# FFN entry of a two-layer hybrid encoder trunk: weight operands 0 to 3 split ahead of the last units, sums of x in another order, first products in two parts

## The reference, cut to what matters

```python
def _swiglu(x, w_in, w_out):
    g, u = jnp.split(x @ w_in, 2, axis=-1)
    return (jax.nn.silu(g) * u) @ w_out

# for each of two layers, x is 512 prompt rows and 8 x 16 sample rows of 1024
x = x + 0.5 * _rmsnorm(_swiglu(_rmsnorm(x, g[0]), w_ffn_in[l, 0], w_ffn_out[l, 0]), g[1])
x = x + _rmsnorm(Mixer_l(_rmsnorm(x, g[2])), g[3])
x = x + 0.5 * _rmsnorm(_swiglu(_rmsnorm(x, g[4]), w_ffn_in[l, 1], w_ffn_out[l, 1]), g[5])
```

## Time and profile before

| | |
|---|---|
| median of 3 runs | 2647.21 us (2640.1 to 2655.18) |
| profiled execution, own time | 2651.45 us |
| its span | 2649.5 us |
| TensorE matmul busy | 2458.7 us (93%) |
| VectorE busy | 1714.9 us (65%) |
| ScalarE busy | 1194.7 us (45%) |
| mean granted TensorE clock | 0.966 of full |

### The profile page before, as it was taken

One profiled execution on the slowest core, in us unless ns is written; L12 is line 12 of the kernel. 1 busy time (PEld: TensorE's weight loads), 2 busy tenths in 40 slices (PEclk: granted clock), 3 DMA queues, 4 the chain that ended last, 5 costly groups with the idle time before them and its releaser, 6 DMA issues.

```text
span 2649.5 us, 37614 instructions
## 1 busy us (share of the span) xinstructions
PE 2458.7 (93%) x13907; PEld 2197.0 (83%) x13907; DVE 1714.9 (65%) x2819; ACT 1194.7 (45%) x2159; POOL 117.9 (4%) x177
## 2 busy tenths in 40 slices
PE   5999999998899899999989999999997687999998
PEld 4999987976767799988789998777775467999887
DVE  6777647676555877745687774663246858777546
ACT  4445435344344554534555453442233435555444
POOL 1000001100001000000100000100000010000000
PEclk9999999999889999999999999999996889999999
DMA  3333334322203223233432324443251032332335
GB/s 114 90 92 84 98 129 164 104 72 73 76 1 127 64 80 96 80 116 131 150 80 80 96 65 143 139 139 127 68 157 54 1 121 71 90 87 80 109 129 175
DMA packets 259140, 261.89 MB, mean 99 GB/s; under 512 B 25568, under 2 KB 214000, under 8 KB 258977
## 3 DMA queue, kind: packets, MB, share of 16 engines
q1 hardware_dynamic: 254224, 243.83, 30.4%
q0 software_dynamic: 4464, 14.80, 1.6%
q10 hardware_dynamic: 288, 1.10, 0.1%
HBM read 249.11 MB, written 10.58 MB: 98 GB/s over the span
## 4 chain that ended last, share of the span: by engine, by line
PE 77%; DVE 14%; ACT 4%; issue 3%; DMA 1%; POOL 1%; SPq 0%; DVEq 0%; ACTq 0%; POOLq 0%
PE ps L844 12%; PE ps L846 12%; PE ps L845 12%; PE ps L902 5%; PE ps L903 5%; PE ps L904 5%; PE ps L1278 3%; PE ps L1279 2%; PE ps L1280 2%; PE ps L961 2%; PE ps L963 2%; PE ps L962 2%; PE ps L1754 1%; DVE w_all L591 1%; DVE xb L707 1%
## 5 line engine op out<-in xcount | busy, mean ns | idle before, releaser
L844 PE MATMUL ps<-xb,w_all 128*128 128x320 f32 x2400 | 751.2, 313 | 54.7 <-DVE w_all L591 33.9
L845 PE MATMUL ps<-xb,w_all 128*128 128x320 f32 x2400 | 747.9, 312 | 0.0
L846 PE MATMUL ps<-xb,w_all 128*128 128x320 f32 x2400 | 747.8, 312 | 0.0
L844 PEld LDWEIGHTS ps<-xb,w_all 128*128 128x128 f32 x2400 | 456.3, 190 | 62.6 <-issue 46.8
L491 DVE TENSOR_TENSOR w_all<-raw,w_all 128x1024 fp32r<-128x1024 f32 (+1 forms) x204 | 207.9, 1020 | 401.2 <-ACT w_all L501 212.7
L845 PEld LDWEIGHTS ps<-xb,w_all 128*128 128x128 f32 x2400 | 456.4, 190 | 0.0
L846 PEld LDWEIGHTS ps<-xb,w_all 128*128 128x128 f32 x2400 | 456.2, 190 | 0.0
L485 ACT ACTIVATE w_all<-raw 128x1024 fp32r<-128x1024 f32 (+1 forms) x204 | 182.3, 895 | 485.1 <-PE ps L904 260.0
L591 DVE TENSOR_TENSOR w_all<-raw,w_all 128x512 fp32r<-128x512 f32 x404 | 277.8, 690 | 146.9 <-ACT w_all L584 145.9
L584 ACT ACTIVATE w_all<-raw 128x512 fp32r<-128x512 f32 x404 | 253.3, 629 | 182.3 <-PE ps L846 138.9
L902 PE MATMUL ps<-w_all 128*128 128x512 f32 x528 | 205.9, 390 | 0.9 <-DVE w_all L506 0.9
(11 more groups left out here) (355 smaller groups left out, 4002.4 us busy)
## 6 DMA issues: line engine op xcount, KB each, us to landing
raw<-in_w_ffn_out SPq DMA_DIRECT2D x176, 512.0 KB, 3.3
raw<-in_w_ffn_in SPq DMA_DIRECT2D x120, 512.0 KB, 5.0
gain<-in_w_ffn_in SPq DMA_DIRECT2D x56, 512.0 KB, 4.9
raw<-in_w_in_odd SPq DMA_DIRECT2D x56, 256.0 KB, 2.7
raw<-in_w_out_even SPq DMA_DIRECT2D x16, 512.0 KB, 3.5
raw<-in_w_out_odd SPq DMA_DIRECT2D x16, 512.0 KB, 3.4
gain<-in_norm_g POOLq DMA_DIRECT2D x12, 512.0 KB, 7.4
raw<-in_w_in_even SPq DMA_DIRECT2D x24, 256.0 KB, 2.6
```

The source lines that it names most:

```text
L844: nc.tensor.matmul(dst, wl, xh[:, k, :], start=first, stop=False, skip_group_check=True)
L845: nc.tensor.matmul(dst, wh, xl[:, k, :], start=False, stop=False, skip_group_check=True)
L846: mm = nc.tensor.matmul(dst, wh, xh[:, k, :], start=False, stop=(k == HK - 1), skip_group_check=True)
```

## The change

Four things are done at each FFN entry. The gate tiles of pairs 0 and 1 are loaded before both up tiles, operands 0 and 1 are split before the last unit of the matmul in front (k == rows - 2) and operands 2 and 3 beside it (k == rows - 1). T1 is made in three pieces, by token tiles 2, 3 and 4, the last straight from PSUM; T3 goes from ahead of product 4 to step 7, T4 from step 8 to step 9, and s4 of pairs 0 and 1 from step 4 and 5 to steps 8 and 9. ScalarE copies token tile 4 in two halves around the high part of T1. Products of pair 0 multiply by the high part of x first (8 matmuls) and wait for its low part only before the last 4. In FFN 0 lambda and `wf` move to the norms in front, and tile 3 is transposed before product 3 in every FFN.

```diff
-            for c in range(pairs):
-                if name[0] == "A" and c == 2:
+            if name[0] == "A":
+                for which in range(2):
+                    for c in range(2):
+                        tile(c, which)
+                        if name == "A0" and which == 0:
+                            load_x(sp, NP - 1 + c)
...
-            if name == ("P5" if j < 2 else "P2"):
+            if name == ("P7" if j < 2 else "P2"):
                 dve.wait_ge(op_lo, NPROD * f + PLACE["P2", j] + 1)
...
+        def dve_t1(dve, f, t):
+            xt0 = XT["pre%d" % (BEFORE[f] + 1)]
+            c0, c1 = max(t * P, HT) - HT, (t + 1) * P - HT
+            if t == 2:
+                dve.wait_ge(xb_lo_done, 7 * f + 1)
+            if t < NT - 1:
+                dve.wait_ge(xt_hi, xt0 + t + 1)
+                b12 = xs[:, 0:HK, HT + c0:HT + c1]
             else:
+                dve.wait_ge(xt_ps, xt0 + NT)
+                b12 = xt_src(t, 0)[:, 0:HK, :]
+            t1 = nc.vector.tensor_tensor(xs[:, 0:HK, c0:c1], b12, xs[:, 0:HK, c0:c1], ALU.subtract)
+            if t == NT - 1:
+                t1.then_inc(t12_done, 1)
...
+        def dve_first_t(dve, f):
+            dve_first_sums(dve, f, 0)
+            dve_t1(dve, f, 2)
+            dve_first_sums(dve, f, 1)
+            dve_t1(dve, f, 3)
+            dve_operand(dve, f, 4)
+            dve_t1(dve, f, 4)
+            dve_operand(dve, f, 5)
+            dve_s2(dve, f, 0)
+            dve_xb(dve, f, "T1")
+            dve_t2(dve, f)
+            dve_s2(dve, f, 1)
...
-        ACT_X = {4: ["T1"], 6: ["T2"], 8: ["T3"], 10: ["T4"], 12: ["B22"]}
+        X_FRONT = {8: "T3", 10: "T4", 12: "B22"}
...
+            act_operand(act, f, 4)
+            act_operand(act, f, 5)
+            xt0 = XT["pre%d" % (BEFORE[f] + 1)]
+            act.wait_ge(xt_ps, xt0 + NT)
+            nc.scalar.activation(xs[:, HK:, 4 * P:], xt_src(4, HK), ACT.Copy)
+            act_xb(act, f, "T1")
+            nc.scalar.activation(xs[:, 0:HK, 4 * P:], xt_src(4, 0)[:, 0:HK, :], ACT.Copy).then_inc(xt_hi, 1)
+            for i in range(RING, NPROD + RING + 3):
+                if i in X_FRONT:
+                    act_xb(act, f, X_FRONT[i])
                 if 0 <= i - RING < NPROD:
                     act_after(act, f, i - RING)
-                if i < NPROD:
+                if 5 < i < NPROD:
                     act_operand(act, f, i)
+                if i == 6:
+                    act_xb(act, f, "T2")
...
-            for i in range(AHEAD, NPROD + RING + 4):
-                if i == 4:
-                    for j in range(2):
-                        dve_first_sums(dve, f, j)
-                    dve.wait_ge(xt_hi, XT["pre%d" % (BEFORE[f] + 1)] + NT)
-                    dve_t(dve, f, "T1")
-                    dve_t(dve, f, "T3")
-                    dve_xb(dve, f, "T1")
-                if i == 5:
-                    dve_t(dve, f, "T2")
-                if i == 6:
-                    dve_xb(dve, f, "T2")
-                if i == 8:
-                    dve_t(dve, f, "T4")
-                    dve_xb(dve, f, "T3")
+            for i in range(6, NPROD + RING + 4):
                 if i < NPROD:
                     dve_operand(dve, f, i)
                     dve_sums(dve, f, i)
+                if i == 6:
+                    dve_xb(dve, f, "T2")
+                if i == 7:
+                    dve_t3(dve, f)
+                if i == 9:
+                    dve_t4(dve, f)
+                if i in X_FRONT:
+                    dve_xb(dve, f, X_FRONT[i])
...
+                if i == AHEAD - 1:
+                    pe_xt(pe, pre_, 3, 3)
                 if i == AHEAD:
-                    pe_xt(pe, pre_, 3, 3)
                     pe_xt(pe, pre_, 4, 4)
...
+                if j == 0:
+                    for k in range(HK):
+                        wh, wl = hi[:, k * P:(k + 1) * P], lo[:, k * P:(k + 1) * P]
+                        nc.tensor.matmul(dst, wl, xh[:, k, :], start=fresh and k == 0, stop=False, skip_group_check=True)
+                        nc.tensor.matmul(dst, wh, xh[:, k, :], start=False, stop=False, skip_group_check=True)
+                    pe.wait_ge(xb_lo_done, 7 * f + XB_ORDER.index(XOF[name]) + 1)
+                    for k in range(HK):
+                        wh = hi[:, k * P:(k + 1) * P]
+                        mm = nc.tensor.matmul(dst, wh, xl[:, k, :], start=False, stop=(k == HK - 1), skip_group_check=True)
...
+            f = FFN_PRE.get("pre%d" % (p + 1))
+            if f is not None and k == rows - 1:
+                act_operand(act, f, 2)
...
+            if f is not None and k == rows - 2:
+                act_operand(act, f, 0)
+                act_operand(act, f, 1)
+            if f is not None and k == rows - 1:
+                act_operand(act, f, 3)
+                if rows == KD:
+                    act_xb_first(act, p)
```

More of the change, by code:

```diff
@@ L379, in tile @@
                 sp_unit(sp, u0 + 2 * c + which, None, wv[:, :, which * stride + c * P:which * stride + (c + 1) * P])
-            for c in range(pairs):
-                if name[0] == "A" and c == 2:
[L384 to L387, removed]
+            if name[0] == "A":
[4 more added lines that the diff above has]
+                            load_x(sp, NP - 1 + c)
+                f = int(name[1])
+                if f:
+                    sp.wait_ge(m_out, 5 * (BEFORE[f] + 1))
+                sp.wait_ge(tok_ready, READY["pre%d" % (BEFORE[f] + 1)] + NT)
+            for c in range(2 if name[0] == "A" else 0, pairs):
                 tile(c, 0)
-                if name == "A0" and c < 2:
-                    load_x(sp, NP - 1 + c)
                 tile(c, 1)
@@ L606, in dve_first_sums, with dve_s2 @@
             nc.vector.tensor_tensor(a21, a21, a22, ALU.add).then_inc(s1_done, 1)
+        def dve_s2(dve, f, j):
+            a11, a12, a21, a22 = quarters(f, j)
+            dve.wait_ge(op_lo, NPROD * f + PLACE["P5", j] + 1)
+            dve.wait_ge(s3_done, KF * f + j + 1)
+            nc.vector.tensor_tensor(a21, a22, a11, ALU.subtract).then_inc(s2_done, 1)
         def dve_sums(dve, f, i):
@@ new lines, in dve_t2, with dve_t3 @@
+        def dve_t2(dve, f):
+            dve.wait_ge(xb_lo_done, 7 * f + 3)
+            dve.wait_ge(xt_hi, XT["pre%d" % (BEFORE[f] + 1)] + NT)
+            nc.vector.tensor_tensor(xs_quarter(0, 0), xs_quarter(1, 1), xs_quarter(0, 0), ALU.subtract).then_inc(t12_done, 1)
+        def dve_t3(dve, f):
+            dve.wait_ge(t12_done, 2 * f + 1)
+            dve.wait_ge(xt_hi, XT["pre%d" % (BEFORE[f] + 1)] + NT)
+            nc.vector.tensor_tensor(xs_quarter(0, 1), xs_quarter(1, 1), xs_quarter(0, 1), ALU.subtract).then_inc(t34_done, 1)
@@ L840, in pe_pairs_ffn @@
                 xh, xl = xb[:, XB[XOF[name]]], xb[:, XB[XOF[name]] + 1]
[L841 to L846, removed]
+                fresh = name in ("P1", "P2", "P5")
+                if j == 0:
[7 more added lines that the diff above has]
+                        mm = nc.tensor.matmul(dst, wh, xl[:, k, :], start=False, stop=(k == HK - 1), skip_group_check=True)
+                else:
+                    for k in range(HK):
+                        wh, wl = hi[:, k * P:(k + 1) * P], lo[:, k * P:(k + 1) * P]
+                        nc.tensor.matmul(dst, wl, xh[:, k, :], start=fresh and k == 0, stop=False, skip_group_check=True)
+                        nc.tensor.matmul(dst, wh, xl[:, k, :], start=False, stop=False, skip_group_check=True)
+                        mm = nc.tensor.matmul(dst, wh, xh[:, k, :], start=False, stop=(k == HK - 1), skip_group_check=True)
                 mm.then_inc(prod_mm, 1)
@@ L957, in pe_second_group @@
                         pe.wait_ge(m_out, 5 * p + 1)
+                        pe.wait_ge(ss_m_done, 5 * p + 1)
                     for n in range(2):
@@ L1034, in act_norm_first @@
                     act_xt(act, "pre%d" % (p + 1), t, t)
-                    if t == 2:
+                    if f is not None and t == 2 and rows == KF:
                         act_xb_first(act, p)
+            if f is not None and k == rows - 2:
[5 more added lines that the diff above has]
+                    act_xb_first(act, p)
         def act_xb_first(act, p):
@@ L1049, in act_norm_rest @@
             f = FFN_PRE.get("pre%d" % (p + 1))
-            if f is not None:
-                for i in range(AHEAD):
-                    act_operand(act, f, i)
-            elif nxt:
+            if f is None and nxt:
                 for i in range(2):
@@ L1066, in act_norm_rest @@
                 act_hi(act, nxt[0] + 4, None, BW).then_inc(hi_done, 1)
-            act_xt(act, "pre%d" % (p + 1), 4, 4)
+            if f is None:
+                act_xt(act, "pre%d" % (p + 1), 4, 4)
         def act_norm_start(act):
@@ L1124, in dve_norm_first @@
         def dve_norm_first(dve, p, k, rows):
+            f = FFN_PRE.get("pre%d" % (p + 1))
+            if f is not None and k == rows - 1:
```

(18 more changed lines are left out.)

77 lines of the change are left out of this document (34 added, 43 removed).

## The result

The changed kernel takes 2663.9 us (median of 9 runs, 2662.58 to 2667.88) against 2647.21 us (9 runs, 2638.31 to 2655.18): ratio 1.0066, 95% interval 1.0053 to 1.0079. It is slower, by 0.5 to 0.8%. Its profiled execution took 2662.66 us, with a span of 2660.7 and a mean granted clock of 0.962.

What follows compares the result with a forecast made beforehand. TensorE bounds the kernel, except where it idles at FFN entries, which are VectorE lists. Product 8's +10.3 us and the clock's +6.0 make +16.3 on 2651.45, 2667.8; with that execution 4.2 above median, 2663.5 us, range 2645 to 2676.

Steps and rivals of the forecast that it cites:

- List position of product 8: At each FFN entry, product 8 starts 24.3 us behind VectorE's first weight sum, not 20.5: 3.8 us later.
- Start of the lists: When VectorE's list begins at each entry: FFN 0 -5.35 us, FFN 1 -1.4, FFN 2 +2.55, FFN 3 -0.65.
- The clock: Longer idle time ahead of product 8 brings the low clock to products 8 and 9: +6.0 us over four entries.
- Rival 1: The clock does not fall ahead of product 8, or its fall costs nothing: 2655 us; chance 0.12.
- Rivals 2: VectorE's wait at operand 8 does not form, product 8 moves +2.3 us an entry: 2657 us; chance 0.13.
- The wait at operand 8: VectorE waits 1.5 us for operand 8, which stands behind T3's high part on ScalarE.
- rival 3: The gain at product 4 is kept, since product 6's copy does not hold product 8: 2636 us; chance 0.09.
- Rival 4: Loads come late at FFN 1 and 3, up to 2.55 us each, FFN 0 starts slower: about 2671 us; chance 0.08.
- The price of T1 in pieces: T1 in three pieces on VectorE costs 0.15 us more per entry by the rows, 0.3 by the skill's formula.

Runs made afterwards that it cites:

- e1: Changed kernel with T3 made at step 6, ahead of T2's low part, and T4 at step 7, behind operand 7; ratio 0.9985 to the kernel before.
- e3: Changed kernel with only ScalarE's list altered, the copy of product 6 ahead of T4's high part; ratio 1.0063 to the kernel before.
- e8: Kernel before with only T3, T4 and the late s4 moved later, low parts of T3, T4, B22 behind their step's operand; ratio 1.0112.
- e2: Changed kernel with operands 0 and 1 of FFN 2 behind the last late unit again; ratio 1.0067 to the kernel before.
- e5: Changed kernel with 56 matmuls that nobody reads added between products 7 and 8; ratio 1.0029 to the kernel before.
- e6: e1 and e2 together, plus ScalarE's copies of products 6 and 7 and operand 10 ahead of T4's and B22's high parts; 2633.5 us, ratio 0.9961.
- e9: Changed kernel with T1 in one piece behind the whole copy of token tile 4; ratio 1.0094 to the kernel before.
- e4: Changed kernel with 44 matmuls that nobody reads added between products 7 and 8; ratio 1.0074 to the kernel before.

## Why the prediction was right, point by point

The forecast was 2663.5 us, measured 2663.9. The mechanism held: VectorE's list reaches T4 later, the copy and product 8 wait for it, and the longer idle time costs clock. Its terms, by the same matmuls in both traces:

- **List position of product 8, +3.8 an entry.** Measured 24.27 to 24.28 in FFN 1 to 3 (20.5 before): +3.8, with both waits seen, 1.46 at operand 8 and 1.85 at operand 10 (said: 1.5 and 1.9). e1, e3 and e8 show the cause: T3 and T4 late, and T4 ahead of the copies in ScalarE's list. In FFN 0 it was 27.6, but that list starts at 28.73 and waits for tile 3 and 4; in time, product 8 is 3.0 earlier there (said: 1.6 earlier), part of which the low clock takes: 1.6 is left at product 15. The prediction had product 0 of FFN 0 delayed by 0.55 us, to 26.46; it starts at 25.29, and the last piece of T1 at 36.24 instead of 37.65. Most of that is scatter: the kernels here that share this beginning have product 0 anywhere from 25.10 to 26.41.
- **Start of the lists.** FFN 2: +2.8 (said +2.55), by the DMA wait of 2.98 us ahead of the late unit, shown by e2. FFN 3: -1.5 (said -0.65): ScalarE did wait 0.62 us for the raw tile there, but TensorE's idle time ahead of the last units stayed at 0.73 us (0.72 before), so the unit was not held, a term that I put in and that cost nothing. FFN 1: -1.5 (said -1.4).
- **The clock, +6.0** (the terms as written, 4 x 2.0 - 2 x 1.1, make 5.8). From product 8 on 84 matmuls take 14.30, 14.42, 15.07 and 14.47 us, before 12.81, 12.81, 14.10 and 14.09: +4.5. The term was too large by 1.5, since a fall of the clock cost 1.5, 1.6, 2.3 and 1.7 us against 12.81 and not 2.0 at each entry. e5 removes the idle time and with it 5.7 us of the changed kernel's time. Rival 1 is out: the clock is at 0.55 while TensorE still stands idle, and e5 shows that its fall costs time.
- **What I didn't see, +1.6.** The last units ahead of FFN 2 waited 3.23 us and then ran at the low clock themselves. The window of the 26 matmuls, after:
```profile
1312.61:1319.96 7.35, 7.35 (x26) 5.93 (x27) 2.60 (x4) 1.11 (x2) 0.74 (x2) 0.77 0.24 71
```
and of the kernel before:
```profile
1310.49:1316.26 5.77, 5.77 (x26) 4.76 (x27) 3.66 (x5) 2.67 (x5) 0.74 (x2) 1.00 0.41 116
```
- **The sum.** At product 15 the entries stand at -1.6 (FFN 0; said +0.4), +3.75 (FFN 1; said +4.4), +9.1 (said +7.3) and +2.7 (said +4.0): +13.9 where +16.3 was said. The spans differ by 11.2: another -2.7 arose outside the entries, -2.6 of it around 795 to 805 us, where the kernel before ran at 0.50 and the changed one did not. The window of before, then of after:
```profile
800.00:805.00 5.00, 3.54 (x10) 2.56 (x9) 1.38 (x2) 0.72 (x2) 0.00 (x0) 0.50 0.03 11
...
800.00:805.00 5.00, 5.00 (x24) 4.11 (x23) 0.28 (x1) 1.06 (x1) 0.00 (x0) 1.00 0.01 3
```
No part of the change lies there, and why the clock differed stays open. The medians differ by 16.7. That the forecast hit the median to 0.4 us is luck to some 5 us: for the profiled execution it said 2667.8, and 2662.66 was measured, 5.1 less. What made up for it is that the profiled execution of before was 4.2 us above its median and that of after 1.2 below.
- **Rivals 2, 3 and 4.** The wait at operand 8 formed. The gain at product 4 was not kept: TensorE stands 8.4 us at product 8 instead. Even with T4 sooner (e6) only a part is kept, since VectorE's whole list comes next, a bound that rival 3 did not name. Rival 4 did not come either: the lists of FFN 1 and 3 start 1.5 us earlier, not later.
- **The price of T1 in pieces.** The trace's 0.42 us for 256 elements is what the Trainium skill gives ("VectorE: DVE Perf Modes", section "The TRN2 errata": (N + 151)/0.96 ns). By its statement that a large tile pays the fixed cost once, T1 whole would be the better choice; e9 shows the pieces ahead by 1.0 us an entry.

## What to carry to other kernels

In a chain of in-order queues, follow the piece of work whose wait has no slack (here the copy ahead of product 8) and count what each edit puts ahead of it; an earlier first product only moves the idle time, and a longer idle time can cost once more in the clock. Make the operands of the product that is late first, and check how far behind it the next bound stands before you pay for more. An operation that may wait for a DMA belongs behind the work in the same queue that is ready.

## What the runs showed of the hardware that was not expected

- The length of a gap alone does not tell whether TensorE's clock falls. In the kernel before, the gap of 1.94 us ahead of product 8 left the clock at 1.00 for all 84 matmuls in FFN 0 and 1 (12.81 us each), and in FFN 2 of the same execution it was followed by 0.50 (first window; FFN 3 alike). In FFN 0 of e1 a gap of 3.69 us left it at 1.00 for all 84 (second window), and in e4 one of 2.77 us in FFN 3 did, where one of 2.10 us in FFN 1 was followed by 0.50. The idle times of 8.34 to 9.29 us were followed by the low clock in all four entries.
```profile
1345.00:1347.00 2.00, 2.00 (x10) 2.00 (x9) 2.00 (x4) 1.61 (x3) 0.00 (x0) 0.50 0.00 0
...
52.43:66.00 13.57, 12.79 (x84) 12.29 (x84) 12.83 (x21) 7.27 (x14) 0.00 (x0) 1.00 0.60 155
```
- The Trainium skill ("TensorE: Matmul & The Clock Gate", section "Loop structure matters more than you think") warns of a long wait between matmuls and has 8 us in its example. The rows above show the fall behind gaps well below that, too.
